# A two-block hybrid network on one core: one stage of preparation, the recurrence's heads and the cumulated steps one tile later, and ten tiles with their low weights last

## The reference

```python
hn = rmsnorm(h, norm1_w)
proj = hn @ w_in                     # 1024 x 9760
gates, z, xbc, dt_raw, lru_x, lru_y = split(proj)
# branch one: state-space mixer
xbc = silu(causal_dwconv(xbc))       # 4 taps; x, B and C
dt = softplus(dt_raw + dt_bias)      # 32 heads
cs = cumsum(dt * -exp(a_log))        # the cumulated steps
# branch two: recurrence, 10 blocks of 128 columns
u = causal_dwconv(lru_x)
r_gate, i_gate = sigmoid(u @ w_r + b_r), sigmoid(u @ w_i + b_i)
a_t = exp(-8 * r_gate * softplus(-lam))
b_t = sqrt(1 - a_t**2) * i_gate * u  # then h_t = a_t h_{t-1} + b_t
```

## Time and profile before

| | |
|---|---|
| median of 3 runs | 1235.39 us (1231.95 to 1236.85) |
| the profiled execution, its own time | 1235.14 us |
| its span in the profile | 1233.8 us |
| PE busy | 1191.5 us, 97% |
| DVE busy | 754.8 us, 61% |
| ACT busy | 676.8 us, 55% |
| POOL busy | 347.5 us, 28% |
| mean granted clock of PE | 0.993 |

### The profile page before, as it was taken

How to read it: one execution, slowest core, us unless ns; L and a number is a source line. 1 busy time by engine, 2 the same in 40 slices (tenths; PEclk the granted TensorE clock), 3 DMA queues, 4 the chain that set the end, 5 groups by cost and what they waited for, 6 DMA issues and landing times.

```text
span 1233.8 us, 20584 instructions
## 1 busy us (share of the span) xinstructions
PE 1191.5 (97%) x8552; PEld 1102.7 (89%) x8552; DVE 754.8 (61%) x1018; ACT 676.8 (55%) x932; POOL 347.5 (28%) x211
## 2 busy tenths in 40 slices
PE   9798999999999999999999899999999989999997
PEld 8798999999998999999998699999899877999996
DVE  7878988677455645554878354544456953544444
ACT  5778776686435443434646864444454387544442
POOL 0000000035821111112475533222225673322221
PEclk9899999999999999999999999999999999999999
DMA  9444756534555655554543346665554533666560
GB/s 298 154 135 140 239 177 199 187 125 169 184 193 203 205 195 182 185 191 138 183 136 127 104 151 202 194 193 182 163 180 146 163 103 107 201 201 191 177 200 35
DMA packets 152444, 210.77 MB, mean 171 GB/s; under 512 B 5504, under 2 KB 132640, under 8 KB 151712
## 3 DMA queue, kind: packets, MB, share of 16 engines
q1 hardware_dynamic: 151584, 205.08, 51.9%
q10 hardware_dynamic: 768, 4.39, 1.0%
HBM read 208.37 MB, written 1.08 MB: 170 GB/s over the span
## 4 chain that ended last, share of the span: by engine, by line
PE 78%; ACT 10%; DVE 8%; issue 2%; POOL 1%; DMA 1%; SPq 0%; ACTq 0%; DVEq 0%
PE bank L522 77%; ACT w_hi L975 2%; ACT tmp L975 2%; DVE w_lo L1365 2%; ACT L975 2%; PE bank L530 1%; DVE xbc L1373 1%; ACT probs_dil L975 1%; DMA raw<-in_w_in 1%; POOL w_lo L1937 1%; DVE work L1369 1%; ACT lru_ab L975 0%; ACT xbc L975 0%; ACT probs_dsa L975 0%; DVE lru_u L1373 0%
## 5 line engine op out<-in xcount | busy, mean ns | idle before, releaser
L522 PE MATMUL bank<-act_hi,w_hi 128*128 128x256 f32 (+1 forms) x2040 | 582.1, 287 | 16.8 <-DVE w_lo L1365 12.5
L522 PE MATMUL bank<-act_lo,w_hi 128*128 128x256 f32 (+1 forms) x2040 | 574.3, 283 | 0.0
L522 PE MATMUL bank<-act_hi,w_lo 128*128 128x256 f32 (+1 forms) x2040 | 564.2, 283 | 0.0
L1365 DVE TENSOR_TENSOR w_lo<-raw,w_hi 128x2048 fp32r<-128x2048 f32 (+4 forms) x174 | 366.3, 2106 | 242.6 <-ACT w_hi L975 242.5
L975 ACT ACTIVATE w_hi<-raw 128x2048 fp32r<-128x2048 f32 (+1 forms) x191 | 360.0, 1885 | 252.7 <-PE bank L522 245.2
L522 PEld LDWEIGHTS bank<-act_hi,w_hi 128*128 128x128 f32 (+1 forms) x2040 | 390.8, 192 | 26.6 <-issue 19.9
L522 PEld LDWEIGHTS bank<-act_lo,w_hi 128*128 128x128 f32 (+1 forms) x2040 | 391.1, 192 | 2.1 <-issue 0.5
L522 PEld LDWEIGHTS bank<-act_hi,w_lo 128*128 128x128 f32 (+1 forms) x2040 | 385.1, 192 | 0.0
L1937 POOL TENSOR_TENSOR w_lo<-raw,w_hi 128x512 fp32r<-128x512 f32 (+1 forms) x146 | 201.1, 1406 | 436.2 <-ACT w_hi L975 436.2
L1937 POOL TENSOR_TENSOR act_lo<-tmp,act_hi 128x512 fp32r<-128x512 f32 x52 | 135.9, 2617 | 431.0 <-ACT act_hi L975 431.0
L522 PE MATMUL bank<-w_hi,act_hi 128*128 128x512 f32 (+1 forms) x536 | 203.0, 379 | 8.3 <-POOL act_lo L1937 5.7
(11 more groups left out here) (232 smaller groups left out, 801.9 us busy)
## 6 DMA issues: line engine op xcount, KB each, us to landing
raw<-in_w_in SPq DMA_DIRECT2D x64, 1024.0 KB, 5.3
raw<-in_w_up SPq DMA_DIRECT2D x32, 1024.0 KB, 5.7
raw<-in_w_down SPq DMA_DIRECT2D x32, 1024.0 KB, 4.9
raw<-in_w_ffn_in SPq DMA_DIRECT2D x22, 1024.0 KB, 5.1
raw<-in_w_out SPq DMA_DIRECT2D x12, 1024.0 KB, 4.9
raw<-in_w_ffn_out SPq DMA_DIRECT2D x11, 1024.0 KB, 4.9
raw<-in_w_out_ssm SPq DMA_DIRECT2D x8, 1024.0 KB, 4.9
raw<-in_w_out_lru SPq DMA_DIRECT2D x5, 1024.0 KB, 4.9
```

Source lines behind the costliest of these rows:

```text
L522: return mm_ops.matmul(out, lhs, rhs, start=start, stop=stop, skip_group_check=True)
L1365: return ops.tensor_tensor(out, a, b, op)
```

## The change

Two edits. The constant LOW_LAST goes from 6 to 10, so tiles 6 to 9 (bc 0 to 3) take columns_low_last. In stage_order gates_ready goes from lx 2 to lx 3; the heads, two at a time, from lx 3, lx 4, bc 0, bc 1 to lx 4, bc 0, bc 1, bc 2, and the last two, which stood alone at bc 2 and bc 3, both to bc 3; dt_cs from bc 1 to bc 2; dt_turn from bc 3 to xs 0. lru_root and all behind it stay.

```diff
@@ -65,7 +65,7 @@
-LOW_LAST = 6
+LOW_LAST = 10
@@ -189,14 +189,13 @@
-    put("mid", ("lx", 2), ("gates_ready",))
-    for tile, heads in ((("lx", 3), (0, 1)), (("lx", 4), (2, 3))):
-        put("mid", tile, *[("lru", h) for h in heads])
-    put("mid", ("bc", 0), ("lru", 4), ("lru", 5))
-    put("mid", ("bc", 1), ("dt_cs",), ("lru", 6), ("lru", 7))
-    put("mid", ("bc", 2), ("lru", 8))
-    put("mid", ("bc", 3), ("dt_turn",), ("lru", 9))
-    put("mid", ("xs", 0), ("lru_root", 0))
+    put("mid", ("lx", 3), ("gates_ready",))
+    put("mid", ("lx", 4), ("lru", 0), ("lru", 1))
+    put("mid", ("bc", 0), ("lru", 2), ("lru", 3))
+    put("mid", ("bc", 1), ("lru", 4), ("lru", 5))
+    put("mid", ("bc", 2), ("dt_cs",), ("lru", 6), ("lru", 7))
+    put("mid", ("bc", 3), ("lru", 8), ("lru", 9))
+    put("mid", ("xs", 0), ("dt_turn",), ("lru_root", 0))
     put("mid", ("xs", 1), ("lru_root", 1))
```

## The result

The changed kernel takes 1236.88 us (median of 20 runs, 1235.36 to 1238.99), the one before 1235.51 us in the runs taken with it (20, 1231.95 to 1236.85). The ratio is 1.0016, 95% interval 1.0009 to 1.0023: 1.4 us (0.11%) slower as a difference of the medians, 2.0 us (0.16%) by the ratio. Forecast were 1237.2 us and a shift of 1.84. The profiled execution took 1236.84 us, span 1235.5.

A forecast was written before the change was run, and what follows sets the result against it. ACT and DVE queues were taken to bound the kernel up to tile 15, PE from there on. Profiled 1235.14 + 1.84 = 1236.98 us, with the median 0.25 above the profiled run: 1237.2 us, range 1232.5 to 1241.

The forecast's parts named there:

- The bound: First 160 us: ACT and DVE queues set when tile 15 starts; from there PE sets the pace.
- The softplus: DVE starts it 4.54 us later, 2.71 us of ACT work moves ahead: net 1.83 us late.
- Heads, dt_cs, dt_turn: ACT's heads one tile later: tile 12's split 1.84 us late, scan stall unchanged, tile 15 at 124.12.
- Low weights last: Tiles 6 to 9 on PE: earlier starts land in later gaps; worth 0, bounds 0 and 0.
- The gaps of PE and the clock: PE gaps of 3.9 and 6.6 us before tiles 10 and 11; a clock dip takes 1.95, net cost 0.
- B: PE sets the pace all along: its wait and slow clock, 7.8 us, are saved, 1227.6 us; chance 0.08.
- C: Clock stays down in tiles 11 to 14: about 8 us slower, 1243.4 us; chance 0.06.
- D: The 1.84 us disappears in ACT or DVE waits, or PE's waits behind 122 us: 1235.4 us; chance 0.16.

The follow-up runs named there:

- e1: Kernel before with LOW_LAST 10 alone, stages where they were; 1235.28 us, ratio 1.0005.
- e2: Changed kernel with LOW_LAST back at 6, so only the moved stages; 1238.08 us, ratio 1.0019.
- e5: Changed kernel with spare matmuls in PE's idle time ahead of tiles 10 and 11; 1237.54 us, ratio 1.0019.
- e3: Kernel before, with ACT issuing the transfer of the cumulated steps later, after bc 1's convolution is opened; 1231.07 us, ratio 0.9967.
- e9: Kernel before, with one split, w_lo of tile 5, moved from DVE to POOL; 1236.71 us, ratio 1.0014.
- e6: Changed kernel, with ACT issuing the transfer of the cumulated steps after bc 2's convolution is opened; 1232.82 us, ratio 0.9985.

## Why the prediction was right

*The bound.* That tile 15 is the point from which PE sets the pace, and that ahead of it PE is led by ACT and DVE, held in every run: e1, e2 and e5 moved PE's idle time and its clock about and left tile 15 within 0.1 us; e3 took 3.84 us from ACT alone and moved it by 4.0.

*The softplus.* Forecast were 1.83 us; measured were 1.91 at tile 12 and 1.90 at tile 15, with some 0.1 us of it there already at tile 4 (32.74 for 32.63). DVE began it at 47.78 (forecast 47.67), the table load came at 53.76 (53.66). e2 puts the whole price here, e9 shows the rate of one to one from another side.

*Heads, dt_cs, dt_turn.* Heads 2, 6, 8 and the split of tile 12 came within 0.1 us of the forecast. The wait for the scan was 3.84 before and after, as said.

*Low weights last.* Worth nothing: shown by e1 and e2, one on each side.

*The gaps of PE and the clock.* The size was off here. I put the gaps in front of tiles 10 and 11 at 3.9 and 6.6 us and left open whether the first brings the clock down. It was 3.32, as PE began tile 8 only at 63.09, when it was through with tile 7, and not at 62.4; and the clock did come down: it was at 0.50, the 1.2 GHz level, until 87.8, so tile 10 took 3.2 us more (81.66 to 94.32 less the wait of 3.47 is 9.19, not 5.99). I had reckoned 1.95 for a dip, from one whose slow stretch was as long but lay in part in a wait. The 3.2 us filled nearly half of the second gap. Behind that one, 3.47 us long, the slow stretch was the shorter one; tile 11 took 103.03 - 94.32 - 1.23 = 7.48, 1.5 more. Not forecast at all was the wait of 1.82 us in front of tile 5, which PE now reaches earlier. The conclusion stood, since all of it fell into waits; e5 shows no price for the two dips. The Trainium skill (TensorE: Matmul & The Clock Gate, "What's actually happening") has it that the throttled state is the default and activity lifts it. The trace agrees as far as both long gaps were followed by 0.50.

*The rivals.* B needed head 8 below 85; it was at 92.54. The rule of the Trainium skill that stood beside it (Perfetto Trace Analysis, "Optimization Strategy"), to make start sooner what the gaps of the most contended engine wait for, was followed to the letter by the change at tile 6 and gave nothing, because what that gap's w_lo waits for was not made shorter but only dealt out otherwise. Applied to what tile 15 waits for, as in e3, the same rule gave 3.8 us. C needed the slow clock over 5.9 us of loss; it was 4.7 in all, in tiles 10 and 11, and 3.2 of it lay ahead of the stretch I had counted; PE still waited 1.24 us for w_lo in front of tile 15. D is excluded by the starts of tiles 12 and 15.

What stays open: whether a part of the difference lies elsewhere than in the 1.9 us. The medians differ by 1.4, by the ratio and its interval it is 1.1 to 2.8 us, and the rest behind tile 15 varies by more than 3 us between executions. In the two profiled ones it is the same within 0.2 us, with the same 6.8 us of low clock in it. The prediction held that 0.5% is the least that can be told from no change; with 20 runs of each kernel the interval reached 0.07% to either side, enough to tell 0.16% from it.

## What to carry to other kernels

When the busiest engine waits for something that two other engines produce in turn, don't add up its gaps: lay the two queues out instruction by instruction up to the first point from which the busy engine runs through, and compare only that point. Moving a stage in such queues costs or gives the difference between what now stands ahead of it on the one engine and what can fill the wait on the other. And look for an instruction that stands in a queue and waits only to issue a transfer which nobody needs soon: here it was worth twice what the whole change cost.

## What was not expected of the hardware

Small DVE instructions that take 0.15 to 0.41 us took 1.25 to 1.45 us each while POOL ran a split in pieces of 1.33 us, about one POOL piece for one DVE instruction. In the same stretch six convolution instructions took 3.49 us in place of 2.46, though POOL ran beside only part of them. A split moved from DVE to an idle POOL thus cost DVE more than the 2.2 us it relieved it of: ACT's first Exp came 2.12 us later on balance.

The length of a gap did not tell how long the granted clock would be low. It was at 0.50 for 6.8 us with the gap of 5.87 us in the kernel before and with the one of 3.32 us in the changed kernel, and for 3.4 us with the one of 3.47 us. What a slow stretch costs PE depends on how much of it lies in the wait: the two of 6.8 us cost 1.95 and 3.2 us. Nor did the length tell whether the clock falls at all. Behind a wait of 1.83 us in front of tile 5 it was at 0.50 from 41.3 to 44.7 in e2, and at 1.00 in the changed kernel behind a wait of 1.82 us in the same place. Behind waits of 2.73 us in front of tile 12 it fell in e5 and stayed at 1.00 in e6.
